# Output norm, output projection and second norm issued per 128 tokens inside the head-group stage, instead of after it

## The reference, cut to what matters

```python
proj = rmsnorm(x, ln1_g) @ w_in                       # 1024 -> 2560
u, q, fp, i, g, qx = split(proj)
o_pool = pool_mixer(u, ...)                           # 256 columns
o, S   = hgrn2_scan(silu(q), k, i, log_f, S0)         # 4 heads, chunk by chunk
o      = o * rsqrt(mean(o*o, per head) + EPS)         # the output norm
o_hgrn = o * onorm_g * silu(g)                        # 512 columns
o_x    = cross_attn(qx, mem_k, mem_v)                 # 256 columns
x = x + concat([o_pool, o_hgrn, o_x]) @ w_out         # the output projection
h = rmsnorm(x, ln2_g)                                 # the second norm
a, b = split(h @ w_up);  x = x + (gelu(conv(a)) * b) @ w_down
y = rmsnorm(x, lnf_g)
```

## Time and profile before

| | |
|---|---|
| runs | 1357.9 and 1418.43 us, median 1388.16 |
| profiled execution | 1376.79 us, span 1375.8 us (core 1; the cores span 1339.8 to 1375.8) |
| busy share of the span | PE 70%, PEld 39%, DVE 40%, ACT 38%, POOL 7% |
| final chain of waits | PE 47%, DMA 15%, DVE 15%, ACT 13%, issue 8% |
| head-group chunks to first up matmul, tiles 0 to 3 | 65.94, 66.71, 67.37, 65.54 us |

### The profile page before, as it was taken

How to read it: one execution, slowest core, us unless ns; L and a number is a source line. 1 busy time by engine, 2 the same in 40 slices (tenths; PEclk the granted TensorE clock), 3 DMA queues, 4 the chain that set the end, 5 groups by cost and what they waited for, 6 DMA issues and landing times.

```text
span 1375.8 us, 17377 instructions; the slowest of 8 cores (1339.8 to 1375.8 us)
## 1 busy us (share of the span) xinstructions
PE 957.2 (70%) x5823; PEld 537.6 (39%) x5823; DVE 556.0 (40%) x1090; ACT 521.7 (38%) x883; POOL 91.3 (7%) x141
## 2 busy tenths in 40 slices
PE   2294676688984779689467996994779793433565
PEld 1151232236642234276223444841234282321454
DVE  1106344432216446532443564326445532128154
ACT  2335353233235454433553545235454402230242
POOL 1010011110000000000000000000000000210010
PEclk9595689877875689999756998995689996655588
DMA  7998399999860224416303452380134416992574
GB/s 134 241 162 117 111 144 129 141 189 204 279 212 1 92 92 153 169 63 209 128 6 117 123 175 86 108 273 18 34 96 154 168 64 181 260 127 66 165 262 154
DMA packets 94886, 192.81 MB, mean 140 GB/s; under 512 B 12023, under 2 KB 72070, under 8 KB 80688
## 3 DMA queue, kind: packets, MB, share of 16 engines
q0 software_dynamic: 72064, 130.59, 42.5%
q1 hardware_dynamic: 22736, 61.12, 13.0%
HBM read 184.53 MB, written 39.18 MB: 163 GB/s over the span
## 4 chain that ended last, share of the span: by engine, by line
PE 47%; DMA 15%; DVE 15%; ACT 13%; issue 8%; DVEq 1%; ACTq 0%; POOL 0%; SPq 0%; POOLq 0%
PE ps L263 43%; DMA sb_ring<-w_up 6%; DMA sb_kst<-ck 3%; DMA sb_ring<-w_dn 2%; DVE sb_mT L838 2%; ACT sb_QSall L819 2%; DVE sb_hT L331 2%; DVE sb_QSall L821 2%; ACT sb_THall L818 1%; DMA sb_xres<-x_tok 1%; ACT sb_THall L502 1%; ACT sb_K L500 1%; ACT sb_R_sb L667 1%; DMA sb_ring<-w_kv 1%; PE ps L329 1%
## 5 line engine op out<-in xcount | busy, mean ns | idle before, releaser
L263 PE MATMUL ps<-sb_hT,sb_ring 128*128 128x512 bf16 (+2 forms) x2416 | 491.3, 367 | 71.9 <-DMA sb_ring<-w_up 30.2
L263 PEld LDWEIGHTS ps<-sb_hT,sb_ring 128*128 128x128 bf16 x2416 | 228.7, 104 | 329.1 <-issue 149.1
L263 PE MATMUL ps<-sb_ring,sb_mT 128*128 128x256 bf16 x1496 | 177.7, 285 | 27.3 <-ACT sb_hb L318 22.7
L263 PEld LDWEIGHTS ps<-sb_ring,sb_mT 128*128 128x128 bf16 x1496 | 152.1, 102 | 52.7 <-issue 29.3
L818 ACT ACTIVATE sb_THall<-ps 128x512 f32<-128x512 f32 x88 | 52.6, 598 | 228.5 <-DVE sb_THall L817 131.9
L100 POOL DMA_DIRECT2D sb_ring<-wscr x88 | 46.6, 530 | 924.9 <-PE ps L263 856.2
L821 DVE SCALAR_TENSOR_TENSOR sb_QSall<-sb_THall,sb_prm,sb_QSall 128x512 f32<-128x512 f32 x88 | 66.1, 752 | 55.5 <-ACT sb_QSall L819 55.5
L873 DVE TENSOR_TENSOR sb_xres<-ps,sb_xres 128x256 f32<-128x256 f32 x68 | 28.7, 424 | 138.9 <-PE ps L263 138.7
L263 PE MATMUL ps<-sb_ring,sb_mixT 128*128 128x512 bf16 x272 | 69.9, 424 | 16.9 <-DVE sb_mixT L673 14.8
L329 PE MATMUL ps<-sb_idb,sb_hb 128*128 128x128 bf16 x288 | 30.4, 273 | 64.2 <-ACT sb_hb L324 58.7
L819 ACT ACTIVATE sb_QSall<-ps,sb_prm 128x512 f32<-128x512 f32 x88 | 68.4, 778 | 8.8 <-ACT sb_THall L818 0.7
(11 more groups left out here) (175 smaller groups left out, 988.8 us busy)
## 6 DMA issues: line engine op xcount, KB each, us to landing
sb_ring<-wscr POOLq DMA_DIRECT2D x72, 1024.0 KB, 6.2
sb_ring<-wscr POOLq DMA_DIRECT2D x16, 1408.0 KB, 6.5
wscr<-sb_ring SPq DMA_DIRECT2D x18, 1024.0 KB, 6.1
sb_ring<-w_up POOLq DMA_DIRECT2D x22, 512.0 KB, 10.8
sb_xres<-x_tok SPq DMA_DIRECT2D x17, 512.0 KB, 11.9
y_tok<-sb_xres SPq DMA_DIRECT2D x17, 512.0 KB, 5.7
sb_ring<-w_dn POOLq DMA_DIRECT2D x4, 1408.0 KB, 37.8
wscr<-sb_ring SPq DMA_DIRECT2D x4, 1408.0 KB, 10.9
```

What stands on the lines that cost most here:

```text
L263: S.op('pe', lambda e, l=l, r=r, i=i: e.matmul(out_ap, lhsT=l, rhs=r, start=(i == 0), stop=(i == n - 1)), reads=reads, writes=[pskey], inc ...
```

## The change: what it does

- `onorm_chunk(cc)`: the output norm is done for one chunk and all four heads at once (4 × 128 = 512 columns), right after the chunk's state update. The factor `onorm` is now multiplied into `GS` by one more VectorE operation per head in stage 1, so the last product has no scalar.
- `outproj_sub(sub)`: output projection of one sub (both halves, 16 matmuls), its two additions, and its second norm, emitted right behind `onorm_chunk` in one piece, without a step for another generator in between.
- Before each `outproj_sub`, `g_hgrn` steps idly until pool and attention have been emitted to their end.
- `mixT` gets separate keys (`mixTp`, `mixTa`, `mixTh0` to `mixTh3`).
- Both output weight blocks are held until the last sub; the second is taken with `prefetch=False`, so two up loads are issued with the next `wneed()`. POOL's queue has the same loads in the same order.
- `cst_tok` of the decode tile lies in the memory of `S0f`; `osq`, `R`, `t1` are at least 512 wide.

```diff
-        def wneed():
+        def wneed(prefetch=True):
...
-            upto = min(i + NSLOT - 1, len(wseq) - 1)
+            upto = min(i + NSLOT - 1, len(wseq) - 1) if prefetch else i
...
-            def rms_multi(items, gcol, dstT, wr):
+            def rms_multi(items, gcol, dstT, wr, base=0):
...
+                            S.op('dve', lambda e, h=h: e.tensor_scalar(out=GS[:, h, :], in0=GS[:, h, :], scalar1=onorm(h), scalar2=None, op0=ALU.mult), reads=['GS%d' % h, 'prm'], writes=['GS%d' % h])
...
+                def onorm_chunk(cc):
+                    osq, R, t1, osb = B['osq'], B['R'], B['t1'], B['osb']
+                    cs = slice(cc * 128, (cc + 1) * 128)
+                    v3 = lambda ap: ap[:, 0:512].rearrange("p (h t) -> p h t", h=4)
+                    S.op('act', lambda e: e.activation(out=v3(osq), in_=osb[:, :, cs], func=AF.Square), reads=['osb'], writes=['osq'])
+                    p, k = PS()
+                    mmg(p[:, :], k, [(onesb[:], osq[:, 0:512])], ['onesb', 'osq'])
+                    S.op('act', lambda e: e.activation(out=R[:, 0:512], in_=p[:, :], func=AF.Ln, scale=1.0 / 128, bias=epsc), reads=[k, 'small'], writes=['R'])
+                    S.op('act', lambda e: e.activation(out=R[:, 0:512], in_=R[:, 0:512], func=AF.Exp, scale=-0.5), reads=['R'], writes=['R'])
+                    S.op('dve', lambda e: e.tensor_tensor(out=v3(t1), in0=osb[:, :, cs], in1=v3(R), op=ALU.mult), reads=['osb', 'R'], writes=['t1'])
+                    S.op('dve', lambda e: e.tensor_tensor(out=mixT[:, 2:6, cs], in0=v3(t1), in1=GS[:, :, cs], op=ALU.mult),
+                         reads=['t1', 'GS0', 'GS1', 'GS2', 'GS3'], writes=['mixTh%d' % cc])
+
+                def outproj_sub(sub):
+                    if not wo:
+                        wo.append(wneed()); wo.append(wneed(prefetch=False))
+                    for c in range(2):
+                        wsl, wk = wo[c]
+                        wv = w8(wsl)
+                        p, k = PS()
+                        mmg(p[:, :], k, [(mixT[:, kk, sub * 128:(sub + 1) * 128], wv[:, kk, :]) for kk in range(8)], ['mixTp', 'mixTa', 'mixTh%d' % sub, wk])
+                        S.op('dve', lambda e, p=p, c=c: e.tensor_tensor(out=xres[:, sub, c * 512:(c + 1) * 512], in0=p[:, :], in1=xres[:, sub, c * 512:(c + 1) * 512], op=ALU.add),
+                             reads=[k, 'xres%d' % sub], writes=['xres%d' % sub])
+                    rms_multi([(xres[:, sub, :], ['xres%d' % sub], sub * 128)], 110, hT, ['hT'], base=sub)
...
+                        yield
+                        onorm_chunk(cc)
+                        while not (done['pool'] and done['attn']):
+                            yield
+                        outproj_sub(cc)
...
-                    osq, R, t1 = B['osq'], B['R'], B['t1']
-                    for h in range(4):
...
-                for c in range(2):
-                    wsl, wk = wneed()
...
-                rms_multi([(xres[:, sub, :], ['xres%d' % sub], sub * 128) for sub in range(nsub)], 110, hT, ['hT'])
```

More of the change, by code:

```diff
@@ L317, in rms_multi @@
                 for i_, (src, rd, col0) in enumerate(items):
[L318 to L321 removed]
+                    S.op('act', lambda e, i_=i_, src=src: e.activation(out=hbs[(base + i_) % 2][:], in_=src, func=AF.Square, accum_out=stat[:, base + i_:base + i_ + 1]),
+                         reads=rd, writes=['hb%d' % ((base + i_) % 2), 'stat'])
+                S.op('act', lambda e: e.activation(out=stat[:, 4 + base:4 + base + n], in_=stat[:, base:base + n], func=AF.Ln, scale=1.0 / 1024, bias=epsc), reads=['stat', 'small'], writes=['stat'])
+                S.op('act', lambda e: e.activation(out=stat[:, 8 + base:8 + base + n], in_=stat[:, 4 + base:4 + base + n], func=AF.Exp, scale=-0.5), reads=['stat'], writes=['stat'])
                 for i_, (src, rd, col0) in enumerate(items):
[L323 to L325 removed]
+                    hb = hbs[(base + i_) % 2]
+                    S.op('act', lambda e, i_=i_, src=src, hb=hb: e.activation(out=hb[:], in_=src, func=AF.Copy, scale=stat[:, 8 + base + i_:9 + base + i_]),
+                         reads=list(rd) + ['stat'], writes=['hb%d' % ((base + i_) % 2)])
                     p, k = PS()
@@ L413, in do_tile @@
                 kstep(2)
+                done = {'pool': False, 'attn': False}
+                wo = []
+                def onorm_chunk(cc):
[21 more added lines that the diff above has]
+                    rms_multi([(xres[:, sub, :], ['xres%d' % sub], sub * 128)], 110, hT, ['hT'], base=sub)
                 def g_pool():
@@ L473, in g_pool @@
                         yield
-                        S.op('act', lambda e, p=p, c=c: e.activation(out=mixT[:, c, 0:T], in_=p[:, 0:T], func=AF.Identity, scale=pscale(c)), reads=[k, 'prm'], writes=['mixT'])
+                        S.op('act', lambda e, p=p, c=c: e.activation(out=mixT[:, c, 0:T], in_=p[:, 0:T], func=AF.Identity, scale=pscale(c)), reads=[k, 'prm'], writes=['mixTp'])
+                    done['pool'] = True
                     if not sample:
@@ L717, in g_attn @@
                             yield
-                            S.op('dve', lambda e, pO=pO, pr=pr: e.tensor_tensor(out=mixT[:, 6 + pr, 0:T], in0=pO[:, 0:T], in1=Ra[:, 0:T], op=ALU.mult), reads=[kO, 'hb1'], writes=['mixT'])
+                            S.op('dve', lambda e, pO=pO, pr=pr: e.tensor_tensor(out=mixT[:, 6 + pr, 0:T], in0=pO[:, 0:T], in1=Ra[:, 0:T], op=ALU.mult), reads=[kO, 'hb1'], writes=['mixTa'])
                     else:
@@ L764, in g_attn @@
                         yield
-                        S.op('dve', lambda e: e.tensor_tensor(out=mixT[:, 6, 0:128], in0=pO[:, 0:128], in1=Ra[:, 0:128], op=ALU.mult), reads=[kO, 'hb1'], writes=['mixT'])
+                        S.op('dve', lambda e: e.tensor_tensor(out=mixT[:, 6, 0:128], in0=pO[:, 0:128], in1=Ra[:, 0:128], op=ALU.mult), reads=[kO, 'hb1'], writes=['mixTa'])
                         yield
@@ L769, in g_attn @@
                         yield
-                        S.op('dve', lambda e: e.tensor_tensor(out=mixT[:, 7, 0:128], in0=pO[:, 128:256], in1=Rb[:, 0:128], op=ALU.mult), reads=[kO, 'hb0'], writes=['mixT'])
+                        S.op('dve', lambda e: e.tensor_tensor(out=mixT[:, 7, 0:128], in0=pO[:, 128:256], in1=Rb[:, 0:128], op=ALU.mult), reads=[kO, 'hb0'], writes=['mixTa'])
+                    done['attn'] = True
                     yield
@@ L784, in do_tile @@
                 chk('attn')
-                for c in range(2):
-                    wsl, wk = wneed()
-                    wv = w8(wsl)
-                    for sub in range(nsub):
-                        p, k = PS()
-                        mmg(p[:, :], k, [(mixT[:, kk, sub * 128:(sub + 1) * 128], wv[:, kk, :]) for kk in range(8)], ['mixT', wk])
-                        S.op('dve', lambda e, p=p, sub=sub, c=c: e.tensor_tensor(out=xres[:, sub, c * 512:(c + 1) * 512], in0=p[:, :], in1=xres[:, sub, c * 512:(c + 1) * 512], op=ALU.add),
-                             reads=[k, 'xres%d' % sub], writes=['xres%d' % sub])
                 chk('outproj')
-                rms_multi([(xres[:, sub, :], ['xres%d' % sub], sub * 128) for sub in range(nsub)], 110, hT, ['hT'])
                 chk('norm2')
@@ L949, in build @@
             Xs['ahist'] = sbt(sst, "ahist", [128, 22, 16, 2]); Xs['anew'] = sbt(sst, "anew", [128, 22, 16, 2]); Xs['rowb'] = sbt(sst, "rowb_s", [32, 2, 512])
-            cst_tok = sbt(sst, "cst_tok", [32, 2816])
+            cst_tok = Xs['S0f'][:].rearrange("p b h v -> p (b h v)")[0:32, 0:2816]
             def pre1():
                 S.dma('sp', 's3', Xs['sp_tok'][:], spool.rearrange("(h q) c -> q h c", q=120), writes=['sp_tok'])
-                S.dma('sp', 's4', cst_tok[:], sconv[:, :], writes=['cst_tok'])
+                S.dma('sp', 's4', cst_tok, sconv[:, :], writes=['cst_tok'])
                 kload(0)
@@ L987, in pre2 @@
                         S.dma('pool', 's2', Xs['Vs'][:], cv.rearrange("b (mc p) f -> p b mc f", p=128), writes=['Vs'])
-                        S.dma('sp', 's0', Xs['S0f'][:], shgrn.rearrange("b h d v -> d b h v"), writes=['S0f'])
+                        S.dma('sp', 's0', Xs['S0f'][:], shgrn.rearrange("b h d v -> d b h v"), writes=['S0f', 'cst_tok'])
                     yield
```

28 lines of the change are left out of this document (3 added, 25 removed).

## The result

The change is slower. Its median is **1503.25 us** (12 runs, 1494.57 to 1574.98), that of the kernel before 1369.30 (10 runs, 1355.92 to 1418.43); the ratio is 1.0994 with a 95% interval of 1.0953 to 1.1035. The profiled execution took 1494.57 us, its slowest core spans 1493.5 (core 5). The median is inside the forecast range, 15 us under its number, and on the side that it gave 0.94. Some executions take some per cent longer, with the cores of one die or both at a lower granted clock; the medians and ranges in this text contain them, the ratios leave them out.

What follows compares the result with a forecast made beforehand. No one bound; the stage from first key transpose to first up matmul is latency-bound. Profiled 1376.8 + 147 (four prompt tiles) + 8 (weights) − 4 (decode) = 1528, or 1509 on the lower run; middle 1518 us, range 1470 to 1565.

Steps and rivals of the forecast that it cites:

- first transpose to first lot: Prompt tile, first key transpose to the first 16 output projection matmuls: 24.7 us, uncertain by 1.5 either way.
- a lot: One sub's 16 output projection matmuls on TensorE: 5.95 us, starting at clock 0.50; ends 3.5 and 6.8.
- lot to transposes: Second norm of a sub, last projection matmul to its transposes: 4.27 us, TensorE waiting; then transposes 1.02.
- Rival 1: The clock stays up in the new order: 16 lots at 3.5 instead of 5.95 us, −39, giving 1479; chance 0.08.
- the chunk between: Each of chunks 1 to 3, from a sub's transposes to the next projection: 10.65 us, three times 31.9.
- the end, transposes to up matmul: End of a prompt tile: last `hT` product to first up matmul 1.5 us, 0.1 before it, 1.6; transposes 1.02.
- Weights in tile 0: Both output blocks held to the end, so an up weight block comes later and up projection waits: +8 us; ends 0, +16.
- Decode norm: Decode tile: one norm step replaces four that delay the attention scores, −4 us; ends −5 and 0.
- `cst_tok`, forecast 0: Memory reuse in the decode tile: readers of `cst_tok` end long before `S0f` is loaded, so 0 us.
- Tile 0 absorbs: Rival: tile 0 absorbs its share, loads getting ahead while the stage lasts longer: −45 us, giving 1473; chance 0.04.
- Even: Rival: serial chains and savings even out within 2%, a tile's stage within 7 us of 66; chance 0.02.
- Faster by overlap: Rival: next chunk's work fills TensorE's gaps, −20.6 us a tile, −82 in all, 1295 from the profiled execution; chance 0.04.

Runs made afterwards that it cites:

- second norm lagged: The change, with each sub's transposes and product into `hT` emitted behind the next chunk's state matmuls: median 1463.46 us, about 1.052 of the kernel before (lower two runs only).
- filler: The change, plus unread matmuls in TensorE's waits once attention is over (8 before transposes, 6 before and behind each norm matmul): 1476.00 us, 1.0816 of the kernel before.
- `cst_tok` elsewhere: The change, with `cst_tok` laid into the memory of `S0b` instead of `S0f`: 1496.72 us, 1.0945 of the kernel before.
- norm per chunk: The change without its per-sub projection and idle wait, only the output norm done per chunk: 1399.86 us, 1.013 of the kernel before.
- idle wait: The kernel before, with only the recurrence stepping idly after chunk 0 until pool and attention are emitted: 1384.75 us, 1.015 of the kernel before.
- second order: Against the change: norm matmul, norm products and transposes emitted later, projection by sub after all chunks, attention among chunks, `cst_tok` in `S0b`: 1307.37 us, 0.9589 of the kernel before.
- the three parts: Norm per chunk, idle wait, and projection per sub behind all generators, each run without the other two: 5.7, 6.6 and 16.0 us more per prompt tile than the kernel before.
- projection per sub, behind all generators: The kernel before, with only output projection and second norm done sub by sub after all chunks, norm by head, no idle wait: 1433.78 us, 1.0521 of the kernel before.

## Why the prediction was right, and where its sizes were off

**The mechanism.** The forecast rested on one place, that on TensorE the next chunk stands behind a sub's transposes and these behind its lot. The trace shows it (idle +48.5 us before the transposes), and moving just these transposes gives back 16.2 us a tile. "It did each once" before, four times now, is what the groups' idle times say.

**Prompt tiles, forecast +147, measured +129.3** (395.2 against 265.9). By the steps, in tile 1, forecast first:
- first transpose to first lot 24.7, measured 23.5 (24.8, 23.9 and 25.6 in the other tiles): right.
- a lot 5.95, measured 5.1 to 5.3. The starting clock was right; it rises earlier than in the earlier trace rows, where I had taken the past to be the same. This is the largest miss of the sum, 2.9 us a tile. With the second norm lagged, lots that start at 0.50 take 5.0 to 6.4 us, so one lot of before was a thin base for the length.
- lot to transposes 4.27, measured 4.1 to 4.4; transposes 1.02, measured 0.61 here, as the clock had not yet fallen. Rival 1 had been argued against with just that 1.02; the argument did not carry over, its conclusion on the lots did.
- the chunk between 10.65, measured 10.3. Lot to lot 21.9, measured 20.1 to 20.6.
- the end, transposes to up matmul, 2.6 with the transposes, measured 2.2.

**Weights in tile 0, forecast +8: not told from 0.** The stretch behind the first up matmul is 220.0 us in the change against 221.1 and 220.7 in the two profiles of before, as means of the cores, and TensorE's waits for up weights in it sum to 20.1 against 18.8 and 18.9. The later issue is real; on the profiled core the first such wait comes earlier (24 us behind the first up matmul, 34 before) but is short, 0.69 us against 3.68 in the earlier trace rows, so the sign that I had named, a longer first wait, did not come. I can't call the end "0" of my bounds right either. In the profiles of three kernels with the change's order of weights the stretch is 223.2, 223.7 and 224.4 us (second norm lagged, filler, `cst_tok` elsewhere), and in those of two with the order of before 211.3 and 213.4 (norm per chunk, idle wait), where it takes back what the longer stage of tile 0 costs; the four kernels with the projection behind the generators, which hold both blocks too, show 215.0 to 219.1. These are one execution each, and the cores of one execution differ by up to 31 us. Whether the held blocks cost some us here stays open. The earlier trace rows came from a core on which these loads are slow.

**Decode norm, forecast −4: −6.4.** One step for four saves a little more than the earlier trace rows show.

**`cst_tok`, forecast 0: +6.** This step failed. I had said that its readers end long before `S0f` is loaded. They end before `S0f` is used; but its load used to be issued 0.65 us behind that of `cst_tok`, and now has to wait for them, 14.8 us.

**The base and the sum.** 1518 is a base of 1367 us and +151. The base was right within 2 us of the median that ten runs gave later, 1369.30. Of the +151, the stretches of the cores show 128: 18 less from the stages, 9 less from tile 0's stretch, 2 less from the decode norm, 6 more from the transfer. That the number came within 15 us is in part luck: the stretches lie 23 us under my terms and the medians only 17, and the 6 us between the two are in no stretch that I read. The medians differ by 134. The sum of 1528 on the profiled execution's own time would have been further off, because its slowest core had a tile 0 that was 20 us longer than the mean of the cores.

**Rivals.** *The clock stays up*: no, lots begin at 0.50; with it forced up for three lots of four, the filler run gives 24 to 27 us back, where the price was 39 for all four. The rule that gaps between matmuls let the clock fall (Trainium skill, "TensorE: Matmul & The Clock Gate", "Loop structure matters more than you think") agrees with the trace, and is worth that much here. *Tile 0 absorbs*: no (99.7 us of stage and 220.0 behind it, against 66.0 and 220.7). *Even*: no. *Faster by overlap*: not in this order, for the reason given, that TensorE can't start the scores of chunk 1 before the transposes of sub 0. But in "second order" it is faster, by 4.1%. So the advice to interleave regimes (Trainium skill, "Perfetto Trace Analysis", "Optimization Strategy") holds for this stage: what failed was the order, not the idea. The bound that I gave for it, 20.6 us a tile, was 13.1 in the best run.

**Still open:** the 4.0 us a tile that the three parts cost only together; what the held output blocks cost in tile 0; which wait takes up the 7 us of the late `S0f` load.

## What to carry to other kernels

Interleaving two dependent chains on engines that work in order gained nothing here as long as a chain's next step was written right behind the step it waits for: write it one stage later, behind the other chain's work, and do so on every engine that it passes, VectorE and ScalarE too. Before forecasting, read for each moved instruction what it waits for and what stands right behind it on its queue. And a buffer that is laid over another's memory must be free when the load is issued, not when the data are used.

## What the runs showed of the hardware, unexpected

- The granted clock stays at 1.00 through some 4 us in which TensorE idles behind a lot (476 to 479 in the change), so that the transposes run at full speed (0.61 us for eight), yet it is 0.50 when the next lot begins 11 us later. Behind waits of the same length (4.1 to 4.4 us) the eight transposes take 0.95 to 1.01 us in "projection per sub, behind all generators", and 1.02 in the kernel before, where the clock is 0.50 in the window from 487 to 489.
- Tile 0's stretch with the float32 weight loads takes 205.6 to 236.4 us on the cores of one execution of the kernel before, and 209.5 to 240.5 on those of another, while those of tiles 1 and 2 agree within about 1 us. A single core's timeline is a poor base for a sum that has this stretch in it.
